# The four gate sections of a two-layer decoder trunk, summed over partitions as two rounded products instead of one fp32 product

## The chip, the cores and the metric

The kernel runs on one core of one Trainium2 chip. The metric is the device time of one execution in microseconds; lower is better. A comparison of two kernels is a comparison of such times on the same chip.

## What is computed

A trunk of two layers over 256 positions of width 2048. Layer 0 has dilated window attention in three head groups, layer 1 has differential attention on a key/value set made once between the layers; each layer ends in a squared-ReLU MLP. Every sub-layer is conditioned: its shift, scale and gate are a vector times a 2048-wide matrix of 2048 columns (a *section*).

```python
c_act = jax.nn.silu(c)
for layer in range(DEPTH):
    mod = c_act @ ada_w[layer] + ada_b[layer]
    shift_t, scale_t, gate_t, shift_m, scale_m, gate_m = jnp.split(mod, N_MOD, axis=-1)
    h = modulate(rms_norm(x, norm_g[layer, 0]), shift_t, scale_t)
    ...
    x = x + gate_t[:, None, :] * y
    h = modulate(rms_norm(x, norm_g[layer, 1]), shift_m, scale_m)
    x = x + gate_m[:, None, :] * sq_relu_mlp(h, mlp_w1[layer], mlp_w2[layer])
```

The change concerns the four gates: `gate_t` and `gate_m` of each layer.

## The kernel before

**The weight stream.** All weights of the large products pass through the core once, in pieces of 256 rows by 512 columns, six slots deep (`SLOTS`). SyncE loads a piece into `w_raw` once TensorE has freed the slot. ScalarE rounds it to the reduced fp32 format (`w_hi`, `split` of ScalarE, L811), VectorE subtracts to get the remainder (`w_lo`, which takes the place of `w_raw`, `split` of VectorE, L1131). TensorE multiplies (`gemm`): for each of two row tiles of the activations and each 128 rows of the piece, three products of 512 columns, high by high, high by low and low by high (L383 to L385). A *chunk* is 512 output columns, eight pieces (four in the output projection of layer 0). Here *split j* is the one of piece j of its chunk.

**The sections.** A section is 16 loads of 128 by 2048 (`ada_raw`, two slots). VectorE multiplies each by a column of `c_act` and adds it into `acc` (`ada_piece`, L1142 for the first, L1145 for the others). What is left is the sum of `acc` over its 128 partitions. For a gate, TensorE does that with a product by a matrix of ones (`ones`, `sum_rows`, L522), in four quarters of 512 columns that alternate between two PSUM banks, `tr0` and `tr1`. The result stands on all partitions; VectorE adds it to the bias in `gate` (`move_rows`, L1223), which frees the bank for the quarter after the next. The first load of the next section overwrites `acc`.

**The order** is written out by hand. On each engine a chunk takes a table from a step number j to extra work: ScalarE and VectorE do the steps of j ahead of split j, TensorE does those of j behind piece j. An engine works strictly in its order. There are four places with gate sums, called here by their stage:

- *Output projection, layer 0.* TensorE sums all four quarters behind piece 0 of the first chunk. VectorE masks the last four score tiles in steps 1 to 4 (`mask_scores`, L1270), then splits the attention output into high and low (`low_of_heads`, L1342), for which TensorE waits ahead of piece 0, and then moves the four quarters.
- *MLP, layer 0.* TensorE sums two quarters behind piece 5 and two behind piece 6 of the second chunk; VectorE moves them in steps 1 and 2 of the third. In step 7 of the second chunk ScalarE and VectorE split the hidden activations (`mid`).
- *Key/value section, u = 1.* TensorE computes a score tile behind each of the pieces 0 to 3 (`scores`, L542 and L543) and sums two quarters behind piece 1, right after that piece's scores, and two behind piece 2. VectorE masks the tiles in steps 4 to 7 and moves two quarters in step 6 and two in step 7. TensorE's next score tile waits until the one before has been masked. ScalarE copies the values of the chunk before (`values`, L873 and L874) in step 4. The exponentials start when all four tiles are masked.
- *MLP, layer 1.* As in layer 0, behind pieces 5 and 6 of the fourth chunk.

## Time and profile before

| | us |
|---|---|
| median of 3 runs | 2538.7 |
| lowest and highest | 2536.68 and 2541.55 |
| the profiled execution, its own time | 2537.78 |
| its span, first to last instruction | 2536.0 |
| TensorE busy | 2433.8 (96%) |
| VectorE busy | 1837.7 (72%) |
| ScalarE busy | 1196.1 (47%) |
| DMA, mean over the span | 262 GB/s |

TensorE is busy nearly throughout, VectorE and ScalarE have gaps. A timeline row gives start, duration, engine, line, operation and how many instructions were merged; a bracket gives how long the engine sat idle ahead of it and what released it. TensorE's matmuls overlap, so one of them is recorded with 0.39 us while the next starts 0.23 us after it: what a matmul costs is read from starts, not from durations. A true fp32 product is recorded as two matmuls.

### The profile page before, as it was taken

How to read it: one execution, taken by the hardware profiler on the slowest of the kernel's cores; microseconds unless marked ns; L12 is line 12 of the kernel's file. 1: busy time of each engine (PE TensorE's matmuls, PEld its weight loads, DVE VectorE, ACT ScalarE, POOL GpSimd, SP SyncE). 2: the span in 40 equal slices, each digit the busy share in tenths (PEclk: the TensorE clock that was granted, in tenths of full speed). 3: DMA queues.
4: the chain of work that ended last, by engine and by line, in shares of the span. 5: the costliest groups of instructions: out<-in, count | busy, mean ns of one | idle time of the engine just before them, and what ended most of it. 6: DMA issues, size and time to landing. Idle time of an engine off the chain costs nothing.

```text
span 2536.0 us, 28504 instructions
## 1 busy us (share of the span) xinstructions
PE 2433.8 (96%) x11153; PEld 2001.7 (79%) x11153; DVE 1837.7 (72%) x2223; ACT 1196.1 (47%) x1974; POOL 67.6 (3%) x106
## 2 busy tenths in 40 slices
PE   6899999988999999999999999989899999999999
PEld 5787888867888888888887777767788888888887
DVE  7778888868888777787787778777796555555554
ACT  3255565546443443444446654463643443443442
POOL 2000000011000000000001000000100000000000
PEclk9899999999999999999999999999999999999999
DMA  8878887956897787787786777767695555555554
GB/s 343 342 279 305 294 300 274 357 205 235 320 347 278 283 299 256 285 305 250 286 320 232 267 280 287 277 232 271 241 368 198 191 184 190 191 184 191 190 186 171
DMA packets 150485, 665.27 MB, mean 262 GB/s; under 512 B 16880, under 2 KB 17360, under 8 KB 120912
## 3 DMA queue, kind: packets, MB, share of 16 engines
q1 hardware_dynamic: 150352, 663.46, 71.4%
q8 instruction: 88, 1.44, 0.2%
q14 instruction: 45, 0.37, 0.0%
HBM read 661.30 MB, written 2.10 MB: 262 GB/s over the span
## 4 chain that ended last, share of the span: by engine, by line
PE 69%; DVE 15%; ACT 7%; DMA 5%; issue 3%; SPq 0%; POOL 0%; ACTq 0%; DVEq 0%
PE main L383 20%; PE main L385 20%; PE main L384 20%; DVE w_lo L1131 5%; DVE acc L1145 4%; ACT w_hi L811 2%; DMA ada_raw<-ada 2%; DMA w_raw<-w 2%; DMA qT<-ada 1%; PE tr L468 1%; PE main L397 1%; PE main L399 1%; PE main L398 1%; ACT st_a L851 1%; DVE acc L1162 1%
## 5 line engine op out<-in xcount | busy, mean ns | idle before, releaser
L811 ACT ACTIVATE w_hi<-w_raw 128x1024 fp32r<-128x1024 f32 x800 | 841.5, 1059 | 994.2 <-DMA w_raw<-w 991.5
L1131 DVE TENSOR_TENSOR w_lo<-w_raw,w_hi 128x1024 fp32r<-128x1024 f32 x800 | 970.6, 1222 | 438.8 <-ACT w_hi L811 434.7
L383 PE MATMUL main<-w_hi,hT_hi 128*128 128x512 f32 x1936 | 773.3, 399 | 8.3 <-DVE w_lo L1131 3.6
L385 PE MATMUL main<-w_hi,hT_lo 128*128 128x512 f32 x1936 | 756.0, 390 | 0.0
L384 PE MATMUL main<-w_lo,hT_hi 128*128 128x512 f32 x1936 | 755.3, 390 | 0.0
L383 PEld LDWEIGHTS main<-w_hi,hT_hi 128*128 128x128 f32 x1936 | 364.8, 188 | 87.2 <-DVE w_lo L1131 5.6
L385 PEld LDWEIGHTS main<-w_hi,hT_lo 128*128 128x128 f32 x1936 | 364.2, 188 | 77.7
L384 PEld LDWEIGHTS main<-w_lo,hT_hi 128*128 128x128 f32 x1936 | 364.9, 188 | 74.0 <-issue 1.2
L1145 DVE SCALAR_TENSOR_TENSOR acc<-ada_raw,c_act,acc 128x2048 f32<-128x2048 f32 x165 | 387.3, 2348 | 41.5 <-DMA ada_raw<-ada 40.5
L383 PE MATMUL main<-w_hi,mid_hi 128*128 128x512 f32 x960 | 379.8, 396 | 0.0
L385 PE MATMUL main<-w_hi,mid_lo 128*128 128x512 f32 x960 | 375.7, 391 | 0.0
L384 PE MATMUL main<-w_lo,mid_hi 128*128 128x512 f32 x960 | 373.8, 389 | 0.0
L385 PEld LDWEIGHTS main<-w_hi,mid_lo 128*128 128x128 f32 x960 | 180.2, 188 | 41.8
L384 PEld LDWEIGHTS main<-w_lo,mid_hi 128*128 128x128 f32 x960 | 180.3, 188 | 39.2 <-issue 0.5
L383 PEld LDWEIGHTS main<-w_hi,mid_hi 128*128 128x128 f32 x960 | 180.4, 188 | 37.1 <-issue 0.5
L397 PE MATMUL main<-w_hi,hT_hi 128*128 128x512 f32 x144 | 60.5, 420 | 6.9 <-DVE w_lo L1131 3.4
L945 ACT ACTIVATE st_b<-tr,modc 128x256 f32<-128x256 f32 x56 | 28.3, 555 | 77.5 <-DVE modc L1175 75.3
L399 PE MATMUL main<-w_hi,hT_lo 128*128 128x512 f32 x144 | 57.8, 401 | 0.0
L398 PE MATMUL main<-w_lo,hT_hi 128*128 128x512 f32 x144 | 57.6, 400 | 0.0
L1610 DVE SCALAR_TENSOR_TENSOR st_b<-main,st_a 128x512 f32<-128x512 f32 x64 | 41.1, 684 | 19.0 <-ACT st_a L1066 19.0
L1622 DVE TENSOR_TENSOR mid_lo<-tr,mid_hi 128x512 fp32r<-128x512 f32 x64 | 41.1, 683 | 13.6 <-ACT mid_hi L1076 13.6
L1703 POOL TENSOR_SCALAR st_x<-xs,rstdx 128x256 f32<-128x256 f32 x56 | 44.2, 804 | 174.9 <-PE tr L468 157.6
(222 smaller groups left out, 1755.0 us busy)
## 6 DMA issues: line engine op xcount, KB each, us to landing
w_raw<-w SPq DMA_DIRECT2D x800, 512.0 KB, 3.7
ada_raw<-ada SPq DMA_DIRECT2D x208, 1024.0 KB, 6.2
qT<-ada SPq DMA_DIRECT2D x16, 1024.0 KB, 7.5
gate<-bias_rows SPq DMA_DIRECT2D x4, 1024.0 KB, 7.4
xs<-x SPq DMA_DIRECT2D x1, 2048.0 KB, 7.8
out<-xs SPq DMA_DIRECT2D x3, 512.0 KB, 5.7
out<-xs SPq DMA_DIRECT2D x2, 256.0 KB, 2.5
st_a<-lamb SPq DMA_DIRECT2D x1, 256.0 KB, 9.0
```

The source lines that it names most:

```text
L383: pe.matmul(acc_ps[:, :], hi[:, kt, tc], w_hi[:, s, wc], start=(kt == 0), stop=False)
L384: pe.matmul(acc_ps[:, :], hi[:, kt, tc], w_lo[:, s, wc], start=False, stop=False)
L385: last = pe.matmul(acc_ps[:, :], lo[:, kt, tc], w_hi[:, s, wc], start=False, stop=(kt == PK * pairs - 1))
L397: pe.matmul(acc_ps[:, :], hi[:, kt, tc], w_hi[:, s, wc], start=(kt == 0), stop=False)
L398: pe.matmul(acc_ps[:, :], hi[:, kt, tc], w_lo[:, s, wc], start=False, stop=False)
L399: last = pe.matmul(acc_ps[:, :], lo[:, kt, tc], w_hi[:, s, wc], start=False, stop=(kt == PK * pairs - 1))
L811: act.activation(w_hi[:, s, :], w_raw[:, s, :], ACT.Copy).then_inc(hi_done, 1)
L1131: dve.tensor_tensor(w_lo[:, s, :], w_raw[:, s, :], w_hi[:, s, :].bitcast(F32), ALU.subtract).then_inc(lo_done, 1)
L1145: ins = dve.scalar_tensor_tensor(out=total[:, :], in0=piece, scalar=c_act[:, kt:kt + 1], in1=total[:, :], op0=ALU.mult, op1=ALU.add)
L1610: last = dve.scalar_tensor_tensor(out=stb[:, t, :], in0=main[par][t][:, :], scalar=0.0, in1=sta[:, t, :], op0=ALU.max, op1=ALU.mult)
L1622: dve.tensor_tensor(mid_lo[:, kt:kt + PK, :], tr[kp][:, :].rearrange("p (k n) -> p k n", k=PK), mid_hi[:, kt:kt + PK, :].bitcast(F32), ALU ...
L1703: last = pool.tensor_scalar(dst, src, scale, 1.0, ALU.mult, ALU.mult)
```

## The change

ScalarE copies the whole of `acc` (128 by 2048) into the reduced fp32 format, `acc_hi`, which lies in the free second half of `work`; it waits until the section's last load has been added (`rows_high`). VectorE subtracts it from `acc` in place, `acc_lo` (`rows_low`). TensorE sums each quarter as two products in the reduced format, of `acc_hi` and of `acc_lo`, with rounded ones (`ones_r`, which ScalarE makes once). Ahead of a section's first quarter TensorE waits for `rows_lo` where it waited for `ada_used`.

```diff
+        with nc.sbuf_tensor("acc_lo", [P, D], F32R) as acc_lo:
+            pass
         acc = sb("acc", [P, D])
...
+        acc_hi = work_r[:, D:2 * D]
...
                 def step():
                     if quarter == 0:
                         n["ada"].up(KT)
-                        pe.wait_ge(ada_used, n["ada"].n + ADA_SLOTS)
+                        pe.wait_ge(rows_lo, n["rows"].up())
                     claim_tr(quarter % 2)
-                    pe.matmul(tr[quarter % 2][:, :], ones[:, :], acc_rows[:, quarter, :], start=True,
+                    at = cols(quarter, NC)
+                    pe.matmul(tr[quarter % 2][:, :], ones_r[:, :], acc_hi[:, at], start=True, stop=False)
+                    pe.matmul(tr[quarter % 2][:, :], ones_r[:, :], acc_lo[:, at], start=False,
                               stop=True).then_inc(row_full, 1)
...
+            def rows_high(section):
+
+                def step():
+                    act.wait_ge(ada_used, ADA_SLOTS + KT * (section + 1))
+                    act.activation(acc_hi, acc[:, :], ACT.Copy).then_inc(rows_hi, 1)
+                return step
...
+            act.wait_ge(consts, 2)
             act.wait_ge(vec_done, 1)
...
+            act.activation(ones_r[:, :], ones[:, :], ACT.Copy)
             act.wait_ge(gain_in, 16 * 3)
...
-            chunk(PIECES // 2, {4: [*heads[0:2], values(1), exps(True), move_pt, move_pt, *heads[2:4]]})
+            chunk(PIECES // 2, {2: [rows_high(4)], 4: [*heads[0:2], values(1), exps(True), move_pt, move_pt, *heads[2:4]]})
...
+                    for c in range(1, 5):
+                        rows = [rows_high(13 if final else 5)] if (number, c) == (0, gate_at) else []
+                        chunk(PIECES, {4: [relu(1 - c % 2)], 6: rows, 7: [mid(c - 1)]})
...
-                chunk(PIECES, {4: [values(1)], 8: [exps(False)]})
+                chunk(PIECES, {4: [*([rows_high(10)] if u == 1 else []), values(1)], 8: [exps(False)]})
...
+            def rows_low():
+                dve.wait_ge(rows_hi, n["rows"].up())
+                dve.tensor_tensor(acc_lo[:, :], acc[:, :], acc_hi.bitcast(F32), ALU.subtract).then_inc(rows_lo, 1)
...
-            chunk(0, PIECES // 2, {1: [sc4[0]], 2: [sc4[1]], 3: [sc4[2]],
+            chunk(0, PIECES // 2, {1: [sc4[0]], 2: [sc4[1]], 3: [sc4[2], rows_low],
...
                     if first:
+                        sides[gate_at - 1][7].insert(0, rows_low)
                         sides[gate_at][1], sides[gate_at][2] = all_rows[0:2], all_rows[2:4]
...
                 if u == 1:
+                    side[5].append(rows_low)
                     side[6] += all_rows[0:2]
```

**Key/value section, VectorE.** Split 4, the second masked tile (two parts, each with a row that reads its maximum), and what follows it. Before:

```order
L1131 TENSOR_TENSOR w_lo<-w_raw,w_hi 128x1024
L1268 MEMSET scratch 128x1
L1270 ISA sm,m<-sc,masks 128x128
L1270 ISA m 128x1
L1270 ISA sm,m<-sc,masks 128x256
L1270 ISA m 128x1
L1131 TENSOR_TENSOR w_lo<-w_raw,w_hi 128x1024
```

After:

```order
L1148 TENSOR_TENSOR w_lo<-w_raw,w_hi 128x1024
L1289 MEMSET scratch 128x1
L1291 ISA sm,m<-sc,masks 128x128
L1291 ISA m 128x1
L1291 ISA sm,m<-sc,masks 128x256
L1291 ISA m 128x1
L1248 TENSOR_TENSOR acc_lo<-acc,work_r 128x2048
L1148 TENSOR_TENSOR w_lo<-w_raw,w_hi 128x1024
```

The subtraction over 2048 columns stands behind the second masked tile, ahead of split 5.

**Key/value section, ScalarE.** The splits of pieces 0 to 3, then step 4. Before:

```order
L865 ACTIVATE kT<-tr,gain_cols_sb 128x2x128 x2
L811 ACTIVATE w_hi<-w_raw 128x1024 x4
L873 ACTIVATE vv<-main 128x512
L874 ACTIVATE vv<-main 128x512
L811 ACTIVATE w_hi<-w_raw 128x1024 x4
```

After:

```order
L874 ACTIVATE kT<-tr,gain_cols_sb 128x2x128 x2
L820 ACTIVATE w_hi<-w_raw 128x1024 x4
L967 ACTIVATE work_r<-acc 128x2048
L882 ACTIVATE vv<-main 128x512
L883 ACTIVATE vv<-main 128x512
L820 ACTIVATE w_hi<-w_raw 128x1024 x4
```

The copy over 2048 columns stands ahead of the copies of the values and of split 4.

**Output projection, VectorE.** From the end of the third masked tile, whose last row is left out, to the low parts of the attention output. Before:

```order
L1131 TENSOR_TENSOR w_lo<-w_raw,w_hi 128x1024
L1268 MEMSET scratch 128x1
L1270 ISA sm,m<-sc,masks 128x128
L1270 ISA m 128x1
L1270 ISA sm,m<-sc,masks 128x256
L1270 ISA m 128x1
L1279 TENSOR_TENSOR mn<-m,m_old 128x8
L1280 TENSOR_SCALAR neg<-mn 128x8
L1281 TENSOR_TENSOR diff<-m_old,mn 128x8
L1282 COPY m_old<-mn 128x8
L1342 TENSOR_TENSOR hT_lo<-tr,hT_hi 128x512 x2
```

After:

```order
L1248 TENSOR_TENSOR acc_lo<-acc,work_r 128x2048
L1148 TENSOR_TENSOR w_lo<-w_raw,w_hi 128x1024
L1289 MEMSET scratch 128x1
L1291 ISA sm,m<-sc,masks 128x128
L1291 ISA m 128x1
L1291 ISA sm,m<-sc,masks 128x256
L1291 ISA m 128x1
L1300 TENSOR_TENSOR mn<-m,m_old 128x8
L1301 TENSOR_SCALAR neg<-mn 128x8
L1302 TENSOR_TENSOR diff<-m_old,mn 128x8
L1303 COPY m_old<-mn 128x8
L1363 TENSOR_TENSOR hT_lo<-tr,hT_hi 128x512 x2
```

The subtraction stands between the third masked tile and split 3; the low parts (`hT_lo`) come one row later.

## Rows read from the trace of the kernel before

**Rows 1.** The page, part 4: shares of the chain that ended last, by engine.

```profile
PE 69%; DVE 15%; ACT 7%; DMA 5%; issue 3%; SPq 0%; POOL 0%; ACTq 0%; DVEq 0%
```

**Rows 2.** Timeline, TensorE, layer 0 MLP: start us, us, engine, line, operation, operands, count.

```profile
687.14 1.88 PE L522 MATMUL tr<-acc,ones 128*128 128x512 f32 x4
...
689.55 0.40 PE L383 MATMUL main<-w_hi,hT_hi 128*128 128x512 f32 x1
```

**Rows 3.** Timeline, VectorE, key/value section, u = 1 (idle time before and its releaser in brackets).

```profile
1512.23 2.35 DVE L1145 SCALAR_TENSOR_TENSOR acc<-ada_raw,c_act,acc 128x2048 f32<-128x2048 f32 x1 [0.56 <-DMA ada_raw<-ada]
...
1516.50 1.23 DVE L1131 TENSOR_TENSOR w_lo<-w_raw,w_hi 128x1024 fp32r<-128x1024 f32 x1
1517.65 0.28 DVE L1270 CUSTOM_DVE_ANT_0 sm<-sc,masks 128x128 f32<-128x128 f32 x1
...
1522.54 0.29 DVE L1270 CUSTOM_DVE_ANT_0 sm<-sc,masks 128x128 f32<-128x128 f32 x1 [3.11 <-issue]
...
1523.10 1.28 DVE L1223 TENSOR_TENSOR gate<-tr,gate 128x512 f32<-128x512 f32 x2
```

**Rows 4.** Timeline, ScalarE, the same stretch.

```profile
1514.46 0.58 ACT L873 ACTIVATE vv<-main 128x512 f32<-128x512 f32 x1
...
1515.42 2.94 ACT L811 ACTIVATE w_hi<-w_raw 128x1024 fp32r<-128x1024 f32 x3
```

**Rows 5.** Timeline, TensorE, the same stretch.

```profile
1516.43 0.49 PE L542 MATMUL sc<-kT,qT 128*128 128x128 f32 x2 [1.93 <-DVE m L1270]
...
1517.19 1.88 PE L522 MATMUL tr<-acc,ones 128*128 128x512 f32 x4
...
1521.68 0.38 PE L542 MATMUL sc<-kT,qT 128*128 128x128 f32 x2
...
1523.84 1.98 PE L522 MATMUL tr<-acc,ones 128*128 128x512 f32 x4 [1.34 <-DVE gate L1223]
```

**Rows 6.** Timeline, VectorE, first chunk of the output projection, layer 0.

```profile
545.57 1.22 DVE L1131 TENSOR_TENSOR w_lo<-w_raw,w_hi 128x1024 fp32r<-128x1024 f32 x1
...
547.94 1.28 DVE L1342 TENSOR_TENSOR hT_lo<-tr,hT_hi 128x512 fp32r<-128x512 f32 x2
...
552.70 1.48 DVE L1223 TENSOR_TENSOR gate<-tr,gate 128x512 f32<-128x512 f32 x2 [3.47 <-PE tr L522]
```

**Rows 7.** Timeline, TensorE, the same stretch.

```profile
548.73 0.47 PE L383 MATMUL main<-w_hi,hT_hi 128*128 128x512 f32 x1 [1.23 <-issue]
...
551.57 3.85 PE L522 MATMUL tr<-acc,ones 128*128 128x512 f32 x8
...
555.96 0.39 PE L383 MATMUL main<-w_hi,hT_hi 128*128 128x512 f32 x1
```

**Rows 8.** Timeline, ScalarE, the same stretch.

```profile
538.20 1.06 ACT L811 ACTIVATE w_hi<-w_raw 128x1024 fp32r<-128x1024 f32 x1 [3.97 <-DMA w_raw<-w]
```

**Rows 9.** Timeline, VectorE, layer 0 MLP, around its gate sums.

```profile
678.65 2.35 DVE L1131 TENSOR_TENSOR w_lo<-w_raw,w_hi 128x1024 fp32r<-128x1024 f32 x2
...
688.27 1.48 DVE L1223 TENSOR_TENSOR gate<-tr,gate 128x512 f32<-128x512 f32 x2 [3.80 <-PE tr L522]
```

**Rows 10.** Timeline, ScalarE, the same stretch.

```profile
678.04 1.06 ACT L811 ACTIVATE w_hi<-w_raw 128x1024 fp32r<-128x1024 f32 x1 [0.20 <-DMA w_raw<-w]
```

**Rows 11.** Timeline, VectorE, layer 1 MLP, around its gate sums.

```profile
1921.58 1.48 DVE L1223 TENSOR_TENSOR gate<-tr,gate 128x512 f32<-128x512 f32 x2 [3.34 <-PE tr L522]
```

**Rows 12.** Timeline, TensorE: the first work after the first and the last of six idle times.

```profile
568.91 1.09 PE L468 MATMUL tr<-ident,st_x 128*128 128x128 f32 x4 [5.36 <-POOL st_x L1703]
...
1785.21 1.60 PE L510 MATMUL tr<-ident,acc 128*128 128x128 f32 x8 [2.27 <-DVE sums L1193]
```

**Rows 13.** TensorE by stretch: us, busy (instructions), granted clock, DMA share, GB/s.

```profile
568.00:570.00 2.00, 1.09 (x4) 0.50 0.74 176
...
574.00:576.00 2.00, 2.00 (x9) 0.94 0.03 8
...
1788.00:1790.00 2.00, 2.00 (x8) 0.65 0.00 0
```

More of the change, by code:

```diff
@@ L131, in trunk @@
         xs = sb("xs", [P, T, D])
+        with nc.sbuf_tensor("work_r", [P, 2 * D], F32R) as work_r:
+            pass
         work = sb("work", [P, 2 * D])
@@ L145, in trunk @@
         ones = sb("ones", [P, P])
+        ones_r = sb("ones_r", [P, P], F32R)
         vec = sb("vec", [P, 6, KT])
@@ L227, in trunk @@
         gate_bias = sem("gate_bias")
+        rows_hi, rows_lo = sem("rows_hi"), sem("rows_lo")
         read_out = [sem(f"read_out{p}") for p in range(2)]
@@ L1056, in _, with mlp, block @@
                 chunk(PIECES // 2, {4: [squares_of(c)]})
-            def mlp(final, sections):
+            def mlp(final, sections, gate_at):
                 chunk(PIECES, arrive([squares_of(2)], sections))
-                def block(last=False):
+                def block(number, last=False):
                     def relu(par):
@@ L1079, in mid @@
                         return step
-                    for c in range(1, 4):
-                        chunk(PIECES, {4: [relu(1 - c % 2)], 7: [mid(c - 1)]})
-                    chunk(PIECES, {4: [relu(1)], 7: [mid(3)]})
+                    for c in range(1, 5):
+                        rows = [rows_high(13 if final else 5)] if (number, c) == (0, gate_at) else []
+                        chunk(PIECES, {4: [relu(1 - c % 2)], 6: rows, 7: [mid(c - 1)]})
                     for c in range(1, 4):
@@ L1089, in block @@
                         n["x"].up(4)
-                block()
-                for _ in range(2):
-                    block()
-                block(True)
-            mlp(False, (S_SCALE_M0, S_SHIFT_M0))
+                for number in range(3):
+                    block(number)
+                block(3, True)
+            mlp(False, (S_SCALE_M0, S_SHIFT_M0), 2)
             for ch in range(4):
@@ L1114, in _ @@
                 chunk(PIECES, {4: [squares_of(c)]})
-            mlp(True, (S_SCALE_M1, S_SHIFT_M1))
+            mlp(True, (S_SCALE_M1, S_SHIFT_M1), 4)
         @block.vector
```

## The prediction, made before the changed kernel ran

> **What bounds the kernel now.** I read the page first, then the four places with gate sums in the timeline of each engine. The chain that ended last runs on TensorE for 69% of the span and on VectorE for 15% [rows 1]. So TensorE's own work counts nearly everywhere, and so does whatever it waits for. The reader is to look at each of the four places for two things: what one sum costs TensorE, and whether VectorE is idle there or is what TensorE waits for.
>
> **What a sum costs, before and after.** In the MLP of layer 0 two quarters are four recorded matmuls from 687.14 on. The triples of the weight stream start 0.68 us apart (eleven matmuls in 2.5 us, 0.227 us each); the second triple behind the sum starts at 689.55 [rows 2], so without the sum it would have been at 687.82. Two quarters cost 1.73 us, one quarter 0.86 us. The new form is two products in the format of the weight stream, 2 x 0.227 = 0.45 us. That saves 0.41 us a quarter, 1.64 us a section, 6.6 us in all where nothing waits. This is the whole gain on offer, 0.26% of the time. That the rounded product is no cheaper than the full one can be ruled out: the weight stream runs in this format, at that pace.
>
> The Trainium skill ("TensorE: Matmul & The Clock Gate", section "Back-to-back issue gap") gives 131 ns for a sustained matmul of 512 columns. No row here shows that pace. By it a quarter would cost 0.26 us, and the gain would be near 9.6 us in place of 6.6. I keep the pace of the trace.
>
> **Added work.** Each section gets a copy of 2048 columns on ScalarE and a subtraction of 2048 columns on VectorE. Three copies of 1024 columns take 2.94 us [rows 4], so one of 2048 is about 1.9 us. A VectorE instruction over 2048 columns with two operands takes 2.35 us, and two subtractions of 1024 columns take 2.35 us [rows 3, 9]: 2.3 us. Every copy waits for the last load of its section to be added, and TensorE now waits for the subtraction. The copy of the ones (128 columns, once, at the start) and the wait for constants ahead of ScalarE's first instruction cost nothing: that instruction waits already for a transpose that needs the same constants.
>
> **Key/value section.** Here the new wait lands on the path. The last load has been added at 1512.23 + 2.35 = 1514.6 [rows 3]. ScalarE, which began copying values at 1514.46 and splitting at 1515.42 [rows 4], now copies `acc` from 1514.6 to 1516.5, the values to 1517.5, and does split 4 to 1518.6. VectorE's split 4 began at 1516.50 [rows 3] and so moves by 2.1 us. Behind it come the second masked tile, 1517.65 + 2.1 = 1519.8 to 1520.3, and the subtraction, to 1522.6. TensorE began to sum at 1517.19 [rows 5] and now begins at 1522.7: 5.5 us lost. It has nothing else to do, since the wait stands ahead of piece 2 in its order, and all that is queued behind it waits too: the third score tile, its mask, the two moves, the second pair of sums, the fourth tile, and the exponentials. That sequence is already the path: VectorE idles 3.11 us for the third tile, and TensorE 1.34 us for the first move [rows 3, 5]. So no slack takes the delay, and both pairs of sums give back 0.82 us each on the same path. 5.5 - 1.6 = **+3.9 us**. At the least, even with ScalarE's copy for nothing, the tile's mask (0.6) and the subtraction (2.3) stand between score tile and sum: +1.3 net.
>
> **Output projection.** ScalarE idles 3.97 us up to 538.20 at the point where its copy stands [rows 8], so the copy fits beside VectorE's last addition. But VectorE's subtraction comes at 545.57, ahead of split 3, and the low parts move from 547.94 to 550.2 [rows 6]. TensorE waited for the first of them, 1.23 us idle up to 548.73 [rows 7]; it now waits 2.3 us more. The four quarters cost 3.7 us (551.57 to 555.96, less 0.68 for the triple between [rows 7]), for the third waits until VectorE has moved the first. New: first quarter 0.45, VectorE 0.27 behind it as at 552.70 [rows 6], two moves of 0.69 and 0.6, last quarter 0.45: 2.5 us. 2.3 - 1.2 = **+1.1 us**.
>
> **The two MLPs.** In layer 0 the last load has been added when VectorE starts splits 5 and 6, 678.65 [rows 9]. ScalarE's split 6 (678.04 [rows 10]) begins at 680.7, VectorE's at 681.8, then come the subtraction, the hidden split and two weight splits, until about 688.9. VectorE used to be idle 3.80 us up to its first move at 688.27 [rows 9]. The subtraction ends near 685.3, ahead of TensorE's sum at 687.14. The moves end near 690.2, and the second pair is due at 690.8. It fits, by 0.6 us. In layer 1 VectorE is idle 3.34 us at the same point [rows 11], and the same order holds. 2 x -1.64 = **-3.3 us**. If that cover is short, TensorE waits up to about 1 us in each.
>
> **The clock.** Two stalls grow past what TensorE tolerates here. Behind the start the trace has six idle times of 2.27 us or more; the first is 5.36 us long, the last 2.27 [rows 12]. After each the granted clock is 0.50, the lower of its two levels (1.2 GHz), until about 574.1 after the first, that is 5.2 us after work began again, and until about 1789.4 after the last, 4.2 us after [rows 13]. The shorter ones, 1.93 us at 1516.43 among them [rows 5], left it at 1.0. The idle times here become 1.2 + 2.3 = 3.5 us and 5.5 us. Half of the low time in which TensorE works is lost: 1.7 us where the clock was low for 3.4 us (up to 1789.4), and up to 2.9 us where it was low for twice that, as after the two idle times above 4 us, of which part fell on idle. I take 1.5 us for the first place, as it is nearest to the last of the six, and 2.5 us for the second, which is nearest to the 5.36 us row. **+4.0 us**, bounds 0 and 5.8.
>
> The Trainium skill (the same page, section "HAM oscillation — how this bites in real kernels") states that idle gaps between bursts of matmuls bring TensorE back to half rate, so that the next burst starts slow. It speaks against this change: without the rule the sum would be +1.7, with it +5.7.
>
> **The sum.** 3.9 + 1.1 - 3.3 + 4.0 = +5.7 us. The profiled execution took 2537.78 us, which gives 2543.5; the median of the runs lies 0.9 above it, which gives 2544.4. I say **2544.0**. A measurement of this kernel can tell about 0.2% (5.1 us) from no change, so the forecast lies just beyond that.
>
> **Rivals.**
> 1. *The stalls come, the clock mostly holds.* When the clock falls and returns is not tied to this program's start, so one episode may fall into idle time, or may merge with a later one that is there anyway (the one at 568). For it: the clock was low from 568.0 on, ahead of the work that began at 568.91, so part of that time cost nothing [rows 12, 13]. Against it: six of six. +1.7 with neither, +3.2 with the first alone: 2540 to 2542, within 0.2%, so not slower. It decides if the low time on the two places together is under some 6 us.
> 2. *The covers fail as well.* The copy on ScalarE holds back the hidden split and split 6 in both MLPs, and VectorE's moves come after the second pair is due. +1 each, and both clock losses at their upper bound (+1.8): 2548.
> 3. *The delay is taken up later.* During the stall the loads run ahead; if the 30 us behind it are limited by them and not by the chain, the 5.5 us vanish, and only the savings and the first place are left: 5.7 less 5.5 less the 2.5 of its clock, -2.3; with the first place taken up too, -6.6: 2531 to 2536, faster. For it: VectorE waited 0.56 us for a load just ahead [rows 3]. Against it: behind the sum every idle time is ended by TensorE or VectorE [rows 3, 5], so the loads have caught up there already.
>
> **How the numbers follow.** Forecast 0.52 (2541.5 to 2547; three quarters of it beyond 0.2%), first rival 0.28, second 0.13, third 0.07. Slower by over 0.2%: 0.39 + 0.12 = 0.51. Faster: 0.05. Same: 0.44. The range leaves out most of the third rival and the top of the second: 2537.0 to 2550.0.
>
> **What the profile of the changed kernel would show.** At the key/value section an idle time of some 5.5 us ahead of the first sum with the subtraction as releaser, and a granted clock of 0.5 behind it; in the output projection 3.5 us ahead of piece 0; in the MLPs no idle time ahead of either pair; sums of 0.9 us for two quarters. The forecast is wrong if ScalarE's copy does not delay split 4, if the clock stays at 1.0, or if TensorE waits in the MLPs.

## The result, and the profile after

Over 22 runs of each kernel on the same chip the changed kernel takes **2545.55 us** (median; 2538.59 to 2553.48) and the kernel before 2539.6 us (2533.19 to 2546.03), a ratio of **1.0022** with a 95% interval of 1.0012 to 1.0031. The profiled execution took 2548.45 us, its span is 2546.7 us. The forecast was 2544.0. A later set of 12 runs of the changed kernel (below, `changed_again`) gives 1.0011 (0.9994 to 1.0027). The first interval leaves no loss out, the second just takes it in: the loss is small, 0.1% to 0.3%.

The page of the changed kernel, parts 1 and 4 (busy time and share of the span of each engine; shares of the chain that ended last):

```profile
PE 2434.7 (96%) x11153; PEld 2006.8 (79%) x11153; DVE 1845.2 (72%) x2227; ACT 1203.1 (47%) x1979; POOL 66.4 (3%) x106
...
PE 68%; DVE 16%; ACT 7%; DMA 5%; issue 4%; SPq 0%; POOL 0%; DVEq 0%; ACTq 0%
```

VectorE and ScalarE have taken on some 7 us each, and TensorE's busy time is no shorter although its sums are cheaper. The chain has moved by a point from TensorE to VectorE, and by one to "issue" [rows 1]. Where that happens is to be read at the four places.

**Key/value section.** The timeline of VectorE: last load added, split 4 behind its wait, subtraction. It answers to [rows 3].

```profile
1520.97 2.35 DVE L1162 SCALAR_TENSOR_TENSOR acc<-ada_raw,c_act,acc 128x2048 f32<-128x2048 f32 x1 [1.08 <-DMA ada_raw<-ada]
...
1527.21 1.22 DVE L1148 TENSOR_TENSOR w_lo<-w_raw,w_hi 128x1024 fp32r<-128x1024 f32 x1 [2.10 <-ACT w_hi L820]
...
1528.92 2.29 DVE L1248 TENSOR_TENSOR acc_lo<-acc,work_r 128x2048 fp32r<-128x2048 f32 x1
```

ScalarE in the same stretch: the copy, then the splits from the fourth on. It answers to [rows 4].

```profile
1523.36 1.91 ACT L967 ACTIVATE work_r<-acc 128x2048 fp32r<-128x2048 f32 x1
...
1526.12 3.89 ACT L820 ACTIVATE w_hi<-w_raw 128x1024 fp32r<-128x1024 f32 x4
```

TensorE in the same stretch: second score tile, first pair of sums (each quarter now is a row of L530 and one of L531), the next products, second pair. It answers to [rows 5].

```profile
1525.17 0.49 PE L551 MATMUL sc<-kT,qT 128*128 128x128 f32 x2 [1.85 <-DVE m L1291]
...
1531.26 0.80 PE L530 MATMUL tr<-work_r,ones_r 128*128 128x512 f32 x1 [5.17 <-DVE acc_lo L1248]
1531.86 0.63 PE L531 MATMUL tr<-acc_lo,ones_r 128*128 128x512 f32 x1
...
1533.14 0.63 PE L390 MATMUL main<-w_hi,hT_hi 128*128 128x512 f32 x1
...
1534.42 0.63 PE L390 MATMUL main<-w_hi,hT_hi 128*128 128x512 f32 x1
...
1538.99 0.50 PE L530 MATMUL tr<-work_r,ones_r 128*128 128x512 f32 x1 [1.34 <-DVE gate L1240]
```

Read the three together, from the left edge of each. The last load is in `acc` at 1523.3. ScalarE copies until 1525.2, copies the values, and starts split 4 at 1526.12; VectorE, idle 2.10 us for it, starts its own at 1527.21, and the subtraction at 1528.92. TensorE stands idle from 1526.1 to 1531.26. Behind the wait the triples start 1.28 us apart (1533.14, 1534.42) in place of 0.68: the clock has fallen, and the first pair of rounded sums takes 1.88 us, more than the full one took at the higher clock. The second pair still finds TensorE idle for 1.34 us, exactly as before [rows 5].

TensorE by stretches of 2 us: busy time, number of matmuls, granted clock, DMA share and GB/s. It answers to [rows 13].

```profile
557.00:559.00 2.00, 2.00 (x6) 0.54 0.00 0
...
1528.00:1530.00 2.00, 0.00 (x0) 0.56 0.49 193
...
1532.00:1534.00 2.00, 2.00 (x7) 0.50 0.00 0
...
1536.00:1538.00 2.00, 1.64 (x9) 1.00 0.01 4
```

Both waits that grew are followed by the lower of the clock's two levels: the one in the output projection (first line) and the one here, from 1528 to about 1535.

**Output projection.** VectorE: subtraction, low parts of the attention output, moves [rows 6]. TensorE: piece 0, a triple behind it, the first sum, and the first product behind the last one [rows 7].

```profile
549.27 2.29 DVE L1248 TENSOR_TENSOR acc_lo<-acc,work_r 128x2048 fp32r<-128x2048 f32 x1
...
553.84 1.28 DVE L1363 TENSOR_TENSOR hT_lo<-tr,hT_hi 128x512 fp32r<-128x512 f32 x2
```

```profile
554.63 0.47 PE L390 MATMUL main<-w_hi,hT_hi 128*128 128x512 f32 x1 [3.43 <-issue]
...
556.63 0.63 PE L390 MATMUL main<-w_hi,hT_hi 128*128 128x512 f32 x1
...
559.04 0.39 PE L530 MATMUL tr<-work_r,ones_r 128*128 128x512 f32 x1
...
561.69 0.39 PE L390 MATMUL main<-w_hi,hT_hi 128*128 128x512 f32 x1
```

The idle time ahead of piece 0 grew from 1.23 us to 3.43 us, and the four quarters cost 561.69 - 559.04 = 2.65 us in place of 3.7.

**MLP, layer 0.** VectorE: split 6, subtraction, first moves [rows 9]. TensorE: start of the first pair, the product behind it, and start of the second pair [rows 2].

```profile
688.88 1.23 DVE L1148 TENSOR_TENSOR w_lo<-w_raw,w_hi 128x1024 fp32r<-128x1024 f32 x1 [1.79 <-ACT w_hi L820]
690.02 2.29 DVE L1248 TENSOR_TENSOR acc_lo<-acc,work_r 128x2048 fp32r<-128x2048 f32 x1
...
695.69 1.28 DVE L1240 TENSOR_TENSOR gate<-tr,gate 128x512 f32<-128x512 f32 x2
```

```profile
693.10 0.43 PE L530 MATMUL tr<-work_r,ones_r 128*128 128x512 f32 x1
...
694.13 0.39 PE L390 MATMUL main<-w_hi,hT_hi 128*128 128x512 f32 x1
...
696.87 0.40 PE L530 MATMUL tr<-work_r,ones_r 128*128 128x512 f32 x1
```

Two quarters cost 1.03 us. The subtraction is over at 692.3, TensorE reaches the sum at 693.10 and waits for nothing. VectorE, which sat idle 3.80 us ahead of its first move [rows 9], now arrives at it with no idle time at all. Its two moves end at about 696.4 and 697.0, and the second pair needs the two banks at 696.87 and some 0.5 us later: the cover holds, with 0.4 to 0.5 us to spare. The layer 1 MLP is alike.

**Stage by stage.** The starts of TensorE's products cut the trace into stretches that mean the same in every kernel: each row below runs from the first product of a chunk to the first product of a later one, in us, in one profiled execution of each kernel. (The projection's chunk with the sums is taken from the end of the chunk ahead of it, so that the idle time ahead of piece 0 is in it.) The kernels behind the second column are those of the next section.

| stretch | before | changed | changed_again | kv_only | proj_only | filled | filled_again |
|---|---|---|---|---|---|---|---|
| the first three chunks | 123.57 | 126.76 | 124.87 | 123.61 | 124.87 | 122.83 | 124.07 |
| output projection, chunk with the sums | 34.37 | 38.03 | 37.89 | 35.48 | 38.00 | 35.75 | 36.11 |
| rest of the output projection | 40.39 | 38.54 | 39.90 | 38.41 | 39.85 | 40.40 | 40.50 |
| layer 0 MLP, first two chunks (sums) | 48.83 | 47.33 | 47.23 | 48.89 | 48.89 | 47.23 | 47.23 |
| layer 0 MLP, all chunks behind them | 656.62 | 661.11 | 658.89 | 656.19 | 658.12 | 657.46 | 657.56 |
| key/value chunk with the sums | 31.73 | 37.41 | 39.65 | 37.45 | 31.21 | 35.55 | 35.81 |
| rest of the key/value section | 211.39 | 209.34 | 210.42 | 209.06 | 210.76 | 210.36 | 210.41 |
| layer 1 MLP, four chunks with the sums | 92.23 | 90.66 | 90.66 | 92.24 | 92.24 | 90.66 | 90.66 |

The changed kernel's profile is 10.7 us longer than that of before. Of that 5.7 us are the key/value chunk and 3.7 the projection's, against which the MLPs give 1.5 and 1.6 back, and the stretches behind the two waits 1.9 and 2.0. The rest can't be put down to the change from this profile: 3.2 us are in the start, where no gate is summed, and 4.5 in the layer 0 MLP behind its sums, which has an idle time of 2.96 us at 804 and low clock behind it. A second profile of the same kernel shows 1.3 and 2.3 us there in place of 3.2 and 4.5. Part of the second stretch may be the change's all the same: it is 0.8 to 4.5 us longer than before in every kernel of the table that rounds the MLPs, and 1.5 in `proj_only`; but it is 0.4 shorter in `kv_only`, and 656.46 us, as before, in `all_moved` of experiment 4, which rounds all four places. So one execution doesn't settle a total of 5 us; the runs below come in twelves.

### The profile page after: what moved, and what is told of

The parts are those of the page before. It is cut to its first block, busy times and chain, and to the rows that moved or that the text cites. A ratio compares the mean times of both kernels' runs of the same rounds, so it can differ in the third digit from the quotient of the medians.

```text
span 2546.7 us, 28513 instructions
## 1 busy us (share of the span) xinstructions
PE 2434.7 (96%) x11153; PEld 2006.8 (79%) x11153; DVE 1845.2 (72%) x2227; ACT 1203.1 (47%) x1979; POOL 66.4 (3%) x106
## 4 chain that ended last, share of the span: by engine, by line
PE 68%; DVE 16%; ACT 7%; DMA 5%; issue 4%; SPq 0%; POOL 0%; DVEq 0%; ACTq 0%
PE main L390 20%; PE main L392 20%; PE main L391 20%; DVE w_lo L1148 5%; DVE acc L1162 4%; ACT w_hi L820 2%; DMA w_raw<-w 2%; DMA ada_raw<-ada 2%; DMA qT<-ada 1%; PE tr L475 1%; ACT st_a L860 1%; DVE acc L1179 1%; PE main L404 1%; PE main L405 1%; PE main L406 1%
## 5 line engine op out<-in xcount | busy, mean ns | idle before, releaser
L1495 DVE TENSOR_TENSOR xs<-xs,st_b 128x512 f32<-128x512 f32 x72 | 46.6, 688 | 1.8
```

What stands on the lines that cost most here:

```text
L1495: last = dve.tensor_tensor(xc, xc, stb[:, t, :], ALU.add)
```

## Experiments

**Theory.** The sum of the prediction: the two new waits cost 3.9 and 1.1 us net of the savings, the MLPs give 3.3 us, and the clock takes 4 us behind the two waits. **Rivals:** the waits alone, with the clock indifferent; covers that fail in the MLPs too; a delay that is taken up later.

**1. One part alone.** Only the places in a list are rounded; the others have their full fp32 sum back, without copy and subtraction. The list is [1, 3] in `mlp_only`, [2] in `kv_only` and [0] in `proj_only`:

```diff
+ROUNDED = [1, 3]
...
+                        if n["place"].up() - 1 in ROUNDED:
+                            pe.wait_ge(rows_lo, n["rows"].up())
+                        else:
+                            pe.wait_ge(ada_used, n["ada"].n + ADA_SLOTS)
                     claim_tr(quarter % 2)
+                    if n["place"].n - 1 not in ROUNDED:
+                        pe.matmul(tr[quarter % 2][:, :], ones[:, :], acc_rows[:, quarter, :], start=True,
+                                  stop=True).then_inc(row_full, 1)
+                        return
```

> Rounded products in the two MLPs alone; the output projection and the key/value section sum in full fp32 as before. Theory (both MLP places are covered, stalls lie in the other two): no idle time of TensorE ahead of any gate sum of the MLPs, two quarters cost 0.91 us where they cost 1.73, and the time falls by 3.3 us, ratio 0.9987. Rival (the covers fail, TensorE waits for VectorE in the MLPs too): idle times of about 1 us ahead of the sums, time -1 us to +1 us.

Measured: 2538.6 us, ratio 0.9998 (0.9986 to 1.0010). The interval holds both a gain of 3.3 us and none. The stages decide what the total can't: 47.24 us against 48.83 in layer 0, 90.66 against 92.23 in layer 1. The saving of 1.5 to 1.6 us is there in each place, in every kernel that rounds it, and in none that doesn't. The stretch behind the layer 0 sums is 657.86 us here, 1.2 longer than before, so how much of the saving reaches the total stays open for this kernel.

> Rounded products in the key/value section alone. Theory: TensorE is idle about 5.2 us ahead of its first sum, the granted clock falls to 0.5 behind it, and the time rises by 3.6 us for the wait (5.2 less 1.64) and some 2.5 us for the clock: +6.1 us, ratio 1.0024. Rival (the clock costs nothing): +3.6 us. Rival (the delay is taken up by later waits): 0 or less.

Measured: 2540.42 us, ratio 1.0013 (1.0000 to 1.0025), about 3 us. The chunk takes 37.45 us in place of 31.73, 5.7 more, and what follows it is 2.3 us shorter.

> Rounded products in the output projection of layer 0 alone. Theory: TensorE is idle 3.4 us ahead of piece 0 where it was idle 1.2 us, the sums take 2.5 us less than before's 3.7, clock falls: +1.1 us for the wait and some 1.5 us for the clock, +2.6 us, ratio 1.0010. Rival (the clock costs nothing): +1.1 us. Rival (the wait is hidden by the idle time at the end of the attention): -1.2 us.

Measured: 2541.62 us, ratio 1.0008 (0.9996 to 1.0021). In its profile the chunk takes 38.00 us, 3.6 more, and what follows it 0.5 less. The three totals have the signs that the terms gave them, but are smaller: -0.5 us where -3.3 was expected, +3.3 where +6.1 was, +2.0 where +2.6 was. Each interval reaches some 3 us to either side and holds the theory as well as the first rival (in the key/value section +3.6, nearer to what was measured), so none of them separates the two. For that the clock has to be held up with the waits left in place.

**2. The waits, with TensorE kept busy.** In the two long waits TensorE multiplies weights or activations by the ones into a PSUM bank that the next real product overwrites. The first part below stands ahead of piece 0 of the projection (12 products), the second ahead of the first sum of the key/value section (19). The result is untouched, the waits are as long, and some 0.6 us of idle time is left in each.

```diff
+                    if fill and j == 0:
+                        pe.wait_ge(lo_done, n["w"].n)
+                    for _ in range(fill if j == 0 else 0):
+                        pe.matmul(main[par][0][:, :], ones_r[:, :], w_hi[:, s, 0:NC], start=True, stop=True)
...
+                        if n["rows"].n == 2 and 19:
+                            claim_tr(0)
+                            for _ in range(19):
+                                pe.matmul(tr[0][:, :], ones_r[:, :], hT_hi[:, 0:2, :].rearrange("p k n -> p (k n)"),
+                                          start=True, stop=True)
+                            pe.wait_ge(rows_lo, n["rows"].up())
...
+                gemm(ch % 2, PIECES // 2, hT_hi, hT_lo, ready=ready if ch == 0 else None, fill=12 if ch == 0 else 0,
```

> The changed kernel, with matmuls whose results are overwritten put into TensorE's two long waits: 12 of them (2.7 us) ahead of piece 0 of the output projection, 19 (4.3 us) ahead of the first sum of the key/value section. The waits stay as long; TensorE is no longer idle in them. Theory (low clock behind the waits is a cost of its own, 4.0 us): the granted clock stays at 1.0 in both places, and the time is 4 us under that of the changed kernel, +1.7 us against the kernel before, ratio 1.0007. Rival (the clock behind the waits costs nothing): the time is that of the changed kernel, +5.7 us, ratio 1.0022.

TensorE of `filled` at the two waits:

```profile
546.75 3.05 PE L385 MATMUL main<-w_hi,ones_r 128*128 128x512 f32 x12
550.38 0.50 PE L394 MATMUL main<-w_hi,hT_hi 128*128 128x512 f32 x1 [0.58 <-DVE hT_lo L1376]
...
1515.11 4.78 PE L534 MATMUL tr<-hT_hi,ones_r 128*128 128x512 f32 x19
1520.45 0.50 PE L543 MATMUL tr<-work_r,ones_r 128*128 128x512 f32 x1 [0.57 <-DVE acc_lo L1261]
```

And its granted clock behind them (columns as above):

```profile
550.00:552.00 2.00, 1.62 (x7) 1.00 0.00 0
...
1522.00:1524.00 2.00, 2.00 (x10) 1.00 0.00 0
```

Measured: 2536.09 us, ratio 0.9990 (0.9978 to 1.0002), which is below the kernel before, where the waits net of all savings should leave it above: the interval leaves out both what the theory (1.0007) and what the rival (1.0022) gave. So it and the changed kernel were run again, each beside runs of the kernel before on its own chip.

> The changed kernel with its two waits filled by matmuls, once more. Its first time, 0.999, lies below the 1.0007 that the stages of its profile give (output projection +1.4, key/value chunk +3.8, MLPs -3.2). Theory (the sum of the stages holds): 1.0007, and the key/value chunk again takes 3.8 us more than before. Rival (the filling gives back more than the stages show): 0.999 again.

Measured: 2540.27 us, ratio 0.9999 (0.9988 to 1.0010). That interval holds the 1.0007 of the stages as well as the 0.999 of the first set.

> The changed kernel once more, on the same chip as the others, for its stages. Theory: TensorE takes 5.7 us more from the first to the last product of the key/value chunk with the sums, and 1.8 us more over the output projection, as in its first profile; ahead of the key/value section the first MLP takes as long as in the kernel before (656 to 658 us behind its sums), and the 661 us of the first profile came from a wait that comes and goes. Rival (the first MLP really is longer with the change): 661 us again.

Measured: 2542.49 us, ratio 1.0011 (0.9994 to 1.0027). The expectation on the stages was met in part. The first MLP takes 658.9 us behind its sums, between the two that had been named; the projection takes 3.0 us more than before in place of 1.8, and the key/value chunk 7.9 more in place of 5.7. Of the last, 1.1 us is a longer idle time ahead of the second score tile, where the changed kernel's first profile has 1.85:

```profile
1525.67 0.49 PE L551 MATMUL sc<-kT,qT 128*128 128x128 f32 x2 [2.98 <-DVE m L1291]
```

It ends when VectorE has masked the tile before. That mask comes late where the section's last load or the piece's weights land late, with the change or without it, so the chunks are compared better without this idle time:

| key/value chunk, us | before | mlp_only | proj_only | changed | kv_only | changed_again | filled | filled_again |
|---|---|---|---|---|---|---|---|---|
| chunk with the sums | 31.73 | 31.95 | 31.21 | 37.41 | 37.45 | 39.65 | 35.55 | 35.81 |
| idle ahead of the second tile | 1.93 | 2.15 | 1.38 | 1.85 | 1.85 | 2.98 | 1.94 | 2.20 |
| the rest | 29.80 | 29.80 | 29.83 | 35.56 | 35.60 | 36.67 | 33.61 | 33.61 |
| of it at the lower clock | 0 | 0 | 0 | 6.8 | 6.8 | 10.2 | 0 | 0 |

The last two rows separate the causes. With the clock held up the chunk costs 3.8 us more than before, where the prediction had put the wait net of its savings at 3.9. The low clock adds 2.0 us where it lasts 6.8 us, of which some 3 fall into the wait itself, and 3.1 us where it lasts 10.2: forecast was 2.5. The projection's chunk is 1.4 and 1.7 us longer with filling (forecast 1.1) and 3.7 and 3.5 without, so the clock takes about 2 us there (forecast 1.5; in `kv_only`, which changes nothing there, the chunk is 1.1 us longer, with 3.4 us more of low clock in its heads). The first rival, which has the clock mostly holding, falls for these profiles: idle time replaced by work, at the same place and of the same length, removes the low clock and with it a third to a good half of what each place costs. Over all 24 runs the filled kernel has a mean of 2537.9 us, and the kernel before has 2538.9 over the 87 that ran beside the experiments. That is 1 us below, where the chunks give some 2 us above. Such a mean is uncertain by about 1.7 us (single runs scatter by 3.7 us); the difference stays open.

**3. Where ScalarE's copy stands.** In the key/value section it goes behind split 4 in place of ahead of it, so that it doesn't hold VectorE back.

```diff
-                chunk(PIECES, {4: [*([rows_high(10)] if u == 1 else []), values(1)], 8: [exps(False)]})
+                chunk(PIECES, {4: [values(1)], 5: [rows_high(10)] if u == 1 else [], 8: [exps(False)]})
```

> The changed kernel with ScalarE's copy in the key/value section one step later, behind the copies of the values and split 4. Theory (ScalarE's copy holds back split 4 and so the second mask, 2.1 us of the wait of 5.2): TensorE waits 3.2 us ahead of its first sum, split 4 of VectorE does not wait for ScalarE's copy, and the chunk takes 2 us less than with the change. Rival (the copy has to end ahead of the subtraction anyway, wherever it stands): the wait stays at 5.2 us.

VectorE's subtraction and TensorE's first sum of `kv_copy_late`:

```profile
1520.18 2.29 DVE L1248 TENSOR_TENSOR acc_lo<-acc,work_r 128x2048 fp32r<-128x2048 f32 x1
...
1522.53 0.80 PE L530 MATMUL tr<-work_r,ones_r 128*128 128x512 f32 x1 [3.29 <-DVE acc_lo L1248]
```

Measured: 2541.98 us, ratio 1.0013 (1.0000 to 1.0027). TensorE waits 3.29 us in place of 5.17, and the chunk takes 35.89 us in place of 37.41. The wait is made of the two parts that the prediction had put together, 1.9 us by which the copy holds up split 4, and some 3.3 us for mask and subtraction, which stay. The clock is low behind 3.29 us as it is behind 5.17. The total shows none of this: 1.0013, beside 1.0011 of `changed_again` on the same chip.

The same profile has something else to tell. The projection's wait is as long as in the changed kernel, 3.43 us, but this time the clock held behind it:

```profile
552.28 0.47 PE L390 MATMUL main<-w_hi,hT_hi 128*128 128x512 f32 x1 [3.43 <-issue]
```

```profile
552.00:554.00 2.00, 1.72 (x8) 1.00 0.00 0
554.00:556.00 2.00, 2.00 (x10) 1.00 0.00 0
```

The chunk takes 36.2 us here, as it does with filling (35.75 and 36.11) and some 2 us less than in the changed kernel. So the 2 us are the clock's, with no filling in play, and the first rival's condition, a clock that holds, does occur: in one of the four profiles with this wait.

**4. The same work in idle time.** All four places are rounded, and no filling is added. In the projection VectorE subtracts after the low parts of the attention output, when TensorE has piece 0 to work on. In the key/value section ScalarE copies in step 6, VectorE subtracts at the head of step 6 and makes all four moves in step 7, and TensorE sums behind pieces 4 and 5, after its last score tile.

```diff
-                sums = {1: halves(sum_rows, 1), 3: halves(sum_columns, 1)}.get(u, {})
+                sums = {1: halves(sum_rows, 4), 3: halves(sum_columns, 1)}.get(u, {})
...
-                chunk(PIECES, {4: [*([rows_high(10)] if u == 1 else []), values(1)], 8: [exps(False)]})
+                chunk(PIECES, {4: [values(1)], 6: [rows_high(10)] if u == 1 else [], 8: [exps(False)]})
...
-            chunk(0, PIECES // 2, {1: [sc4[0]], 2: [sc4[1]], 3: [sc4[2], rows_low],
-                                   4: [sc4[3], running_max(1), *lows[0:2], *all_rows, lambda: ada_piece(0), move_pt,
+            chunk(0, PIECES // 2, {1: [sc4[0]], 2: [sc4[1]], 3: [sc4[2]],
+                                   4: [sc4[3], running_max(1), *lows[0:2], rows_low, *all_rows, lambda: ada_piece(0), move_pt,
...
-                    side[5].append(rows_low)
-                    side[6] += all_rows[0:2]
-                    side[7] += all_rows[2:4]
+                    side[6].insert(0, rows_low)
+                    side[7] += [negate_max, *all_rows]
+                    side[8] = []
```

> All four sections as rounded products, with the added work put where the engines are idle. Output projection: VectorE subtracts behind the low parts of the attention output, ahead of the moves. Key/value section: ScalarE copies in step 6, VectorE subtracts at the start of step 6, TensorE sums behind pieces 4 and 5, VectorE moves all four quarters in step 7, behind the last mask and the negated maximum. Theory (the loss of the change is only where its waits stand): no new idle time of TensorE in any of the four places; output projection -1.0 us, key/value section -3.0 us (two pairs of sums at 0.82 less, and the 1.34 us wait for a move gone), MLPs -3.3 us: -7.3 us, ratio 0.9971. Rival (the rounded sums do not shorten the chain, their savings are taken up by later waits): within 2 us of the kernel before, ratio 0.999 to 1.001.

VectorE of `all_moved`, in the projection (subtraction, first moves) and in the key/value section (the same):

```profile
547.69 2.28 DVE L1248 TENSOR_TENSOR acc_lo<-acc,work_r 128x2048 fp32r<-128x2048 f32 x1
550.87 1.29 DVE L1240 TENSOR_TENSOR gate<-tr,gate 128x512 f32<-128x512 f32 x2 [0.90 <-PE tr L531]
...
1516.37 2.29 DVE L1248 TENSOR_TENSOR acc_lo<-acc,work_r 128x2048 fp32r<-128x2048 f32 x1
...
1524.38 1.29 DVE L1240 TENSOR_TENSOR gate<-tr,gate 128x512 f32<-128x512 f32 x2 [2.43 <-PE tr L531]
```

TensorE of the same kernel: piece 0 of the projection, and the first sum of the key/value section with the first product behind its pair.

```profile
547.28 0.47 PE L390 MATMUL main<-w_hi,hT_hi 128*128 128x512 f32 x1 [1.23 <-issue]
...
1523.64 0.40 PE L530 MATMUL tr<-work_r,ones_r 128*128 128x512 f32 x1
...
1524.57 0.39 PE L390 MATMUL main<-w_hi,hT_hi 128*128 128x512 f32 x1
```

Measured: 2530.81 us, ratio **0.9970** (0.9955 to 0.9985). TensorE's idle time ahead of piece 0 is 1.23 us again, as before the change [rows 7]; in the key/value section the sum begins with no idle time, 5.0 us after the subtraction has ended, and VectorE is the one that waits (2.43 us). The chunk takes 28.52 us, 3.2 less than before the change and 8.9 less than with it: to the savings comes that the second pair no longer waits for a bank. The work added to ScalarE and VectorE is the same copies and subtractions. The loss came from where it stood, not from what it is. Of the 7.3 us some 1.3 are that wait for a bank, which the later place removes by itself; full fp32 sums at the later place were not run. The clock has no part in the gain: the mean granted clock of the 12 runs is 0.9891, as before.

**5. The clock as a cost of its own.** To see what the low clock costs where this change has no part, the two longest idle times of the kernel before were filled in the same manner, 18 products ahead of a transpose in the heads of layer 0 [rows 12, first row] and 15 at the start of the key/value section. Then the same was done to `all_moved`.

```diff
+                        if fill_at == j:
+                            for _ in range(18):
+                                pe.matmul(tr[j % 2][:, :], hT_hi[:, 0, 0:P],
+                                          hT_hi[:, 0:2, :].rearrange("p k n -> p (k n)"), start=True, stop=True)
                         pe.wait_ge(staged, n["staged"].n)
...
-            def qk_transposes():
+            def qk_transposes(fill=0):
+                if fill:
+                    claim_tr(0)
+                    for _ in range(fill):
+                        pe.matmul(tr[0][:, :], hT_hi[:, 0, 0:P], hT_hi[:, 0:2, :].rearrange("p k n -> p (k n)"),
+                                  start=True, stop=True)
                 pe.wait_ge(roped, n["roped"].up())
```

> The kernel before, its gate sums untouched, with matmuls whose results are overwritten in its own two longest idle times behind the start: 18 (4.1 us) in the 5.36 us ahead of the third transpose of the output projection, 15 (3.4 us) in the 4.36 us ahead of the transposes at the start of the key/value section. No wait ends earlier. Theory (low clock behind an idle time is a cost of its own): the granted clock stays at 1.0 behind both, where it was 0.5 for 6.8 us each, and the time falls by 4 to 5.5 us, ratio 0.998 to 0.9984. Rival (the low time is covered by other waits): ratio 1.000.

TensorE of `before_filled` at both fillings:

```profile
568.20 4.34 PE L486 MATMUL tr<-hT_hi 128*128 128x512 f32 x18
573.71 0.65 PE L468 MATMUL tr<-ident,st_x 128*128 128x128 f32 x4 [1.17 <-POOL st_x L1713]
...
1478.85 3.56 PE L534 MATMUL tr<-hT_hi 128*128 128x512 f32 x15
1483.38 1.09 PE L541 MATMUL tr<-ident,st_a 128*128 128x128 f32 x8 [0.97 <-DVE st_a L1260]
```

Its clock behind the first of them:

```profile
574.00:576.00 2.00, 1.17 (x9) 0.80 0.91 365
576.00:578.00 2.00, 2.00 (x7) 0.50 0.92 373
578.00:580.00 2.00, 2.00 (x8) 0.84 0.01 4
```

Measured: 2534.36 us, ratio **0.9980** (0.9971 to 0.9989). The second filling removed its low clock altogether. The first didn't, half against what I had expected: 1.17 us of idle time and the pauses around the transposes are left, and the clock still fell, only for a shorter time (from about 575 to 579). So 5 us are to be had from the clock alone, with both waits left where they are.

> The version with the added work moved to idle stretches, and the same two fillings as in the run of the kernel before. Theory: both gains add up, -7.3 and -4 to -5.5: ratio 0.995 to 0.9956. Rival (one gain takes the place of the other): ratio 0.997, as without the fillings.

TensorE of `moved_filled` at its second filling, and its clock behind the first:

```profile
1471.55 3.56 PE L543 MATMUL tr<-hT_hi 128*128 128x512 f32 x15
1476.07 1.09 PE L550 MATMUL tr<-ident,st_a 128*128 128x128 f32 x8 [0.97 <-DVE st_a L1281]
```

```profile
572.00:574.00 2.00, 2.00 (x6) 0.50 0.72 291
574.00:576.00 2.00, 2.00 (x10) 0.93 0.00 0
```

Measured: 2526.59 us (6 runs), ratio **0.9949** (0.9934 to 0.9964). The two gains add up: 0.9970 times 0.9980 is 0.9950. This is the fastest version found, and it beats both kernels.

**6. The clock over all runs.** Every run has a mean granted clock of its own. Over the 87 runs of the kernel before that ran beside the experiments (three chips, with means of 2538.7, 2538.9 and 2539.3 us), time and clock go together with a correlation of -0.77: the two runs at 0.986 have a mean of 2550.4 us, those at 0.987 and 0.988 of 2542.1 (21 runs), at 0.989 of 2538.9 (34), at 0.990 of 2536.5 (21), at 0.991 of 2535.2 (8), and the one at 0.992 took 2531.7. The slope is 2453 us for a clock of 1, give or take 450. A mean clock of c over a span S means that the clock was at its half level for 2 x (1 - c) x S; so the slope is about 0.5 us (0.48, between 0.4 and 0.6) lost for each us at the lower level, what halving the pace of an engine that is nearly always busy should cost. The mean clock of the kernel before is 0.98909, that is 55.4 us at the lower level; that of the changed kernel over its 34 runs 0.98685, or 66.9 us. 11.5 us more at 0.48 are 5.5 us, and the two means lie 5.5 us apart (2538.9 and 2544.4; set by set the changed kernel is 5.5 and 4.0 us above the kernel before).

The same sum for each kernel against the runs of the kernel before on its own chip, in us (each difference of means is uncertain by 2 to 3):

| | mean less before's | more low clock | that at 0.48 | what is left |
|---|---|---|---|---|
| changed_again | +4.0 | +8.7 | +4.2 | -0.1 |
| kv_copy_late | +4.4 | +9.2 | +4.4 | 0.0 |
| kv_only | +3.4 | +2.5 | +1.2 | +2.2 |
| proj_only | +3.5 | +3.4 | +1.6 | +1.9 |
| mlp_only | -0.5 | +0.8 | +0.4 | -0.9 |
| filled | -2.1 | -3.4 | -1.6 | -0.5 |
| filled_again | -0.1 | -0.4 | -0.2 | +0.1 |
| all_moved | -7.5 | +0.3 | +0.1 | -7.6 |
| before_filled | -5.2 | -11.8 | -5.7 | +0.4 |

The gain of `all_moved` is no clock at all, that of `before_filled` is nothing else. In the changed kernel the clock is worth the whole loss, but the three kernels with one part each leave 3.2 us together that the clock doesn't explain.

## Why the prediction was right

**The sum of a quarter.** Right. The rounded pair costs 1.03 us (693.10 to 694.13) in the MLP and 0.93 us (1523.64 to 1524.57) in `all_moved` for two quarters, against 0.90 forecast and 1.73 before. The products start 0.23 us apart, as in the weight stream. The 131 ns of the Trainium skill ("TensorE: Matmul & The Clock Gate", section "Back-to-back issue gap") appears in no row of any of these kernels, so the saving by it, 9.6 us, was rightly left aside.

**The added work.** Copy 1.91 us (about 1.9), subtraction 2.29 us (2.3). Both by nearest rows, both right.

**Key/value section.** Right in the mechanism and in each step. TensorE idles 5.17 us (5.5), released by the subtraction. With the clock held up, and without the idle time ahead of the second score tile, the chunk costs 3.8 us more (3.9). `kv_copy_late` shows that the copy did hold back split 4 by its own length. The second pair's saving arrives as said, since the idle time of 1.34 us ahead of it is unchanged.

**Output projection.** Right. 3.43 us of idle time (3.5), the four quarters at 2.65 us (2.5); 2.2 - 1.05 = 1.15 us net (1.1), 1.4 and 1.7 in the chunk with the clock held up.

**The two MLPs.** Right, 1.5 and 1.6 us in place of 1.64 each, and no wait for TensorE in either. The margin had been put at 0.6 us, and the moves end 0.4 to 0.5 us ahead of the second pair. Ahead of the first pair it was less than forecast: in layer 0 the subtraction ends 0.8 us before the sum, not 1.8, for the last load was added later here and ScalarE's copy waited for it until 685.99. The second rival (covers that fail) is out.

**The clock.** Right in the mechanism, too firm in its rule, and low in size. The granted clock fell to 0.50 behind both waits, as the Trainium skill has it ("TensorE: Matmul & The Clock Gate", section "HAM oscillation — how this bites in real kernels"); the trace agrees, with 0.54 at 557 and 0.50 at 1532. But the six of six that the prediction leaned on is a count of one profile. In `kv_copy_late` the clock held behind 3.43 us, and in the twelve profiles together the idle time of 2.33 us that lies at 634 before the change was followed by the low clock in eight and not in four. Less what the filled kernels show, the clock took about 2 us in the projection's chunk (1.5) and 2.0 and 3.1 us in the key/value chunk (2.5). Over all runs the low time is 11.5 us longer, worth 5.5 us where 4.0 had been forecast, near the upper bound of 5.8.

**The waits' net, and the total.** The term that was set too high is what was left of waits and savings, +1.7 us. If the clock accounts for all 5.5 us, it came to nearly nothing: the changed and the filled kernels leave between -0.5 and +0.1 us in the last table. The third rival, a delay that is taken up later, would do that, but the stages don't show it. Behind the grown wait the rest of the key/value section takes 209.3 and 210.4 us against 211.4 before. Most of this is one thing: before the change TensorE idles 2.77 us ahead of a score tile at 1632, and the clock is low behind it. In both profiles of the changed kernel the low clock falls in the chunk ahead and the long idle time is absent. In `mlp_only` and `moved_filled`, which have no grown wait, it is absent as well. So it comes and goes by itself, and whether the grown wait makes its absence more likely isn't shown. Behind the projection's wait nothing can be said either: the stretch takes 38.5 and 39.9 us against 40.4, but 38.4 too in `kv_only`, which changes nothing there. The two errors, 1.5 us too little for the clock and 1.7 too much for the rest, cancel. The total of +5.7 met +5.5 to +6 in the first set of runs and +3 to +4.4 in the second. That the sum was this close owes something to luck.

**What stays open.** By the totals alone the parts can't be told apart at 1 to 2 us, since every run has its own number of episodes of low clock. The split into 5.5 and nearly 0 rests on the fit of time to clock over runs, that into 4 and 1.7 on the stages. The filled kernel's mean, 1 us below before, sides with the first; the three kernels with one part each, 3.2 us above what their clock explains, side with the second. Where the chunks' surplus of 2 us goes in the filled kernel was not traced.

## What to carry to other kernels

Ask of an added operation first in which idle stretch of its own engine it can stand, and only then what it costs: the same copy and subtraction made this kernel 0.1% to 0.2% slower just ahead of the sum that needs them, and 0.3% faster a few steps later. A wait like these, 3.3 to 5.2 us on the TensorE that bounds the kernel, costs its length and then, where the clock falls behind it, about half of the low time in which TensorE works. Whether it falls is no matter of one profile: take several. Where such a wait can't be moved, throwaway products into a bank that is overwritten anyway give that half back; here they ended before the wait did, and the chunks show no cost of their own.

## What the hardware showed that I had not expected

- Much of the run-to-run spread of this kernel is the clock: from 2532 to 2552 us, 0.8%, in step with a mean granted clock of 0.992 down to 0.986, at about 0.5 us for each us at the lower level.
- The length of an episode of low clock does not follow that of the wait. In the two profiles of the changed kernel it was 3.4 and 6.8 us behind the same wait in the projection, and 6.8 and 10.2 us behind that in the key/value section; behind 3.29 us of idle time in `kv_copy_late` it fell for 6.8 us as well.
- Nor is it certain that the clock falls. Behind every idle time above 4 us that was left unfilled it did, in all profiles and leaving out the first 200 us; behind 3.43 us it did in three of four, and behind idle times of 2 to 3 us in some and not in others: it held behind 2.86 us in `moved_filled` and fell behind 1.97 us in the same profile.
- Products whose results are thrown away count as work: with 12, 19 and 15 of them in idle times of 3 to 5 us the clock stayed at 1.00 behind the wait. With 18 in the idle time of 5.4 us in the heads, it still fell, behind a further 1.17 us of idle time and several short pauses, and came back sooner.
